# Late modulation joined to the attention, a gate column copied out, conversions moved: an 8-core hybrid attention and mixture-of-experts block on Trainium2

## The reference, cut to what matters

```python
c_act = silu(c)
mod = c_act @ w_ada + b_ada                  # (B, 6*2048)
sh1, sc1, gt1, sh2, sc2, gt2 = split(mod, 6)
h = rmsnorm(x, g_attn) * (1 + sc1) + sh1
proj = h @ w_in
y_a = mixer_a(proj[..., :4608]) @ w_a_up     # three dilated window attentions
y_b = mixer_b(q, k, v of proj) @ w_b_up      # 16 query heads, 4 key heads, all 4096 keys
gates = sigmoid(proj[..., o4:] + b_gate)
x = x + gt1 * ((gates_a * y_a + gates_b * y_b) @ w_out)
h2 = rmsnorm(x, g_ffn) * (1 + sc2) + sh2
x = x + gt2 * moe(h2)                        # 64 experts, 8 per token, one shared
return rmsnorm(x, g_final)
```

## Time and profile before

| | us |
|---|---|
| median of 3 runs | 6872.43 |
| lowest and highest of them | 6843.43, 7095.51 |
| the profiled execution, its own time | 6879.52 |
| its span, from the first to the last instruction of the slowest core (core 1) | 6877.3 |
| spans of the other cores | 6774.1 to 6874.5 |

### The profile page before, as it was taken

How to read it: one execution, slowest core, us unless ns; L and a number is a source line. 1 busy time by engine, 2 the same in 40 slices (tenths; PEclk the granted TensorE clock), 3 DMA queues, 4 the chain that set the end, 5 groups by cost and what they waited for, 6 DMA issues and landing times.

```text
span 6877.3 us, 64218 instructions; the slowest of 8 cores (6774.1 to 6877.3 us)
## 1 busy us (share of the span) xinstructions
PE 3962.4 (58%) x19194; PEld 1888.4 (27%) x19194; DVE 2186.1 (32%) x3834; ACT 2115.5 (31%) x3327; POOL 484.0 (7%) x607
## 2 busy tenths in 40 slices
PE   0103766765763887897895654555444545436545
PEld 0102333332331333343442322222222222213221
DVE  3444444546553322321213442122212212212212
ACT  0012553544561777784111211111111112112111
POOL 0000000000000000001110000001011101101113
PEclk9999877877886999998997776777776777767766
DMA  7653466465753244246755279899899997999987
GB/s 198 193 180 130 100 118 107 101 131 109 128 122 61 56 78 89 54 87 88 69 51 108 57 154 198 177 178 198 171 187 206 191 190 166 187 195 197 190 169 241
DMA packets 357433, 964.68 MB, mean 140 GB/s; under 512 B 139568, under 2 KB 187696, under 8 KB 336560
## 3 DMA queue, kind: packets, MB, share of 16 engines
q0 software_dynamic: 285232, 692.81, 56.8%
q1 hardware_dynamic: 71552, 263.97, 11.7%
HBM read 1372.53 MB, written 192.73 MB: 228 GB/s over the span
## 4 chain that ended last, share of the span: by engine, by line
DMA 35%; PE 34%; DVE 10%; issue 10%; ACT 7%; PEldq 3%; DVEq 1%; POOLq 0%; POOL 0%; ACTq 0%; PEld 0%; SPq 0%; another core or an unknown queue 0%
DMA idle<-e_bias 22%; PE psum L508 9%; DMA arena<-w_ada 4%; PE psum L1496 4%; PE psum L1467 3%; DMA arena<-w_in 3%; PE psum L956 3%; PE psum L958 3%; PE psum L1048 3%; PE psum L943 3%; PEldq L170 3%; DVE arena L465 2%; DMA arena<-yrows,arena 2%; ACT arena L463 2%; DVE arena L394 2%
## 5 line engine op out<-in xcount | busy, mean ns | idle before, releaser
L508 PE MATMUL psum<-arena 128*128 128x512 bf16 (+1 forms) x3648 | 925.7, 417 | 334.8 <-DVE arena L581 101.9
L1496 PE MATMUL psum<-arena 128*128 128x512 bf16 x1456 | 459.7, 486 | 530.7 <-DVE arena L1485 530.7
L1467 PE MATMUL psum<-arena 128*128 128x512 bf16 x2912 | 647.9, 382 | 12.0 <-ACT arena L1451 10.4
L946 ACT ACTIVATE arena<-psum 128x512 bf16<-128x512 f32 x1024 | 603.4, 597 | 102.3 <-PE psum L943 56.6
L508 PEld LDWEIGHTS psum<-arena 128*128 128x128 bf16 (+1 forms) x3648 | 383.4, 107 | 831.9 <-issue 500.1
L1448 PE MATMUL psum<-arena 128*128 128x128 bf16 x1456 | 169.7, 308 | 698.1 <-issue 545.6
L1471 ACT ACT_TABLE_LOAD x88 | 112.9, 1283 | 1271.7 <-PE psum L1467 1271.7
L956 PE MATMUL psum<-arena 128*128 128x512 bf16 x1024 | 405.1, 396 | 100.0 <-ACT arena L946 99.8
L443 ACT ACTIVATE arena<-arena 128x2048 bf16<-128x2048 f32 x102 | 194.1, 1903 | 727.6 <-DMA arena<-xr 504.7
L958 PE MATMUL psum<-arena 128*128 128x512 bf16 x1024 | 403.9, 394 | 0.0
L943 PE MATMUL psum<-arena 128*128 128x512 bf16 x1024 | 402.7, 395 | 0.0
(11 more groups left out here) (182 smaller groups left out, 4983.0 us busy)
## 6 DMA issues: line engine op xcount, KB each, us to landing
arena<-w POOLq DMA_DIRECT2D x129, 2048.0 KB, 36.5
wcast<-w POOLq DMA_DIRECT2D x63, 2048.0 KB, 13.5
arena<-wcast POOLq DMA_DIRECT2D x63, 2048.0 KB, 40.9
arena<-w_ada SPq DMA_DIRECT2D x128, 768.0 KB, 4.8
arena<-xr SPq DMA_DIRECT2D x78, 1024.0 KB, 6.1
yrows<-arena SPq DMA_DIRECT2D x91, 512.0 KB, 10.9
arena<-w_in POOLq DMA_DIRECT2D x15, 2048.0 KB, 45.9
arena<-w_in POOLq DMA_DIRECT2D x32, 512.0 KB, 7.1
```

Source lines behind the costliest of these rows:

```text
L508: ins = e.matmul(po[0:n, :], lhsT=hT_ap[:, k, 0:n], rhs=wv[:, k, :], start=(k == 0), stop=(k == 15))
L946: P.op("act", lambda e: e.activation(out=ptb[pi], in_=pbank(sbk), func=AF.Exp, scale=SCALE), reads=[PB[sbk]], writes=[ptb_t[pi]])
L1467: ins = e.matmul(pbank(bank), lhsT=xgT[g][:, k, :], rhs=wv_[:, k, :], start=(k == 0), stop=(k == 15))
L1496: ins = e.matmul(pbank(b2), lhsT=hidT[h][:, fc, :], rhs=wv_[:, fc, cs], start=(fc == 0), stop=(fc == 3))
```

## The change

The modulation is cut at the columns: the first 4096 are computed at the start, the other 8192 during the attention of mixer B.

- **At the start** (`mod_first`): 32 chunks of 128 x 2048 (1 MB) in four staging buffers, then a sum of 32 products. The first two own tiles' `produce_a1` stand ahead of it. The own tiles are then produced with `a1` two tiles ahead and no chunk between them.
- **During the attention** (`late_parts`): 16 groups of 512 columns, each 16 parts of 128 x 512 (256 KB), in two staging buffers and two accumulators. The parts are put at 256 per 1000 steps; at every 14th step (`si % 14 == 0`) a finished group is summed by four products in bank 6. `A2` follows after the attention.
- **Conversions**: the 13 of the key tiles are put by tile 23, the 30 of the attention by step 880.
- **Further blocks**: the gate column is copied to `gcol[4]` right after the gather, and the tile `hidT[0]`, in which it lies, is free for the rest.

```diff
-    stg_t = [T("stg0"), T("stg1")]
+    acc = V(BIG, [128, 4096], F32)
+    stg = [V(BIG + 16384 + i * 8192, [128, 2048], F32) for i in range(4)]
+    stg_t = [T("stg%d" % i) for i in range(4)]
...
-    def mod_chunk(half, k, pc):
+    def mod_part(bufs, bufs_t, a, a_t, k, col0, n):
...
+        P.dma("sp", "dx", st, w_ada[k * 128:(k + 1) * 128, col0:col0 + n], writes=[bufs_t[i]])
...
-    def mod_finish(half):
+    def mod_sum(a, a_t, c0, n, bank):
...
-            for j in range(48):
+            for j in range(n):
...
+    def mod_first():
+        for k in range(16):
+            for pc in range(2):
+                mod_part(stg, stg_t, acc[:, pc * 2048:(pc + 1) * 2048], t_acc, k, pc * 2048, 2048)
+        mod_sum(acc, t_acc, 0, 32, 7)
...
+    own_a1 = [produce_a1(xr[1024 + j * 128:1024 + (j + 1) * 128, :], 128) for j in range(2)]
+    mod_first()
     for j in range(8):
-        produce(xr[1024 + j * 128:1024 + (j + 1) * 128, :], 128, hT_own[:, :, j * 128:(j + 1) * 128], hto_t[j])
-        mod_h2_step(8)
+        produce_a2(own_a1[j], hT_own[:, :, j * 128:(j + 1) * 128], hto_t[j])
+        if j + 2 < 8:
+            own_a1.append(produce_a1(xr[1024 + (j + 2) * 128:1024 + (j + 3) * 128, :], 128))
...
-            cast_early(20 + (j + 1) * 13 // 32, [t_kb[j]])
+            cast_early(20 + min(13, (j + 1) * 13 // 23), [t_kb[j]])
...
+    def late_parts(upto, sums):
+        while late[0] < min(upto, 256) and late[0] // 16 < late[1] + 2:
+            cc, k = late[0] // 16, late[0] % 16
+            mod_part(late_stg, late_stg_t, late_acc[cc % 2], late_acc_t[cc % 2], k, 4096 + cc * 512, 512)
+            late[0] += 1
+        if sums and late[1] < late[0] // 16:
+            cc = late[1]
+            mod_sum(late_acc[cc % 2], late_acc_t[cc % 2], 32 + cc * 4, 4, 6)
+            late[1] += 1
...
-            cast_early(33 + (kvh * 256 + si + 1) * 30 // 1024, [ptb_t[si % 4]])
+            cast_early(33 + min(30, (kvh * 256 + si + 1) * 30 // 880), [ptb_t[si % 4]])
+            late_parts((kvh * 256 + si + 1) * 256 // 1000, si % 14 == 0)
...
+    while late[1] < 16:
+        late_parts(256, True)
...
+        P.op("dve", lambda e: e.tensor_copy(out=gcol[4], in_=gate_of(x, xgf)), reads=t_xgf, writes=[gcol_t[4], hidT_t[0]])
...
-        step_D(x, 1, gate_of(x, xgf), t_xgf, y, [xgT_t[0]])
+        step_D(x, 1, gcol[4], [gcol_t[4]], y, [xgT_t[0]])
```

More of the change, by code:

```diff
@@ L384, in mod_chunk @@
         stg_i[0] += 1
[L385 to L388, removed]
+        st = bufs[i]
+        P.dma("sp", "dx", st, w_ada[k * 128:(k + 1) * 128, col0:col0 + n], writes=[bufs_t[i]])
         if k == 0:
[L390 to L396 removed]
@@ L398, in mod_finish @@
-    def mod_finish(half):
-        pm = pbank(7)
+            P.op("dve", lambda e: e.tensor_scalar(out=a, in0=st, scalar1=c_act[:, 0:1], scalar2=None, op0=ALU.mult),
+                 reads=[bufs_t[i], t_cact], writes=[a_t])
+        else:
+            P.op("dve", lambda e: e.scalar_tensor_tensor(out=a, in0=st, scalar=c_act[:, k:k + 1], in1=a, op0=ALU.mult,
+                                                         op1=ALU.add),
+                 reads=[bufs_t[i], t_cact], writes=[a_t])
+    def mod_sum(a, a_t, c0, n, bank):
+        pm = pbank(bank)
@@ L401, in f @@
         def f(e):
             ins = None
-            for j in range(48):
-                ins = e.matmul(pm[:, j:j + 1], lhsT=acc[:, j * 128:(j + 1) * 128], rhs=ones_f[:, 0:1],
+            for j in range(n):
+                ins = e.matmul(pm[:, j:j + 1], lhsT=a[:, j * 128:(j + 1) * 128], rhs=ones_f[:, 0:1],
                                start=True, stop=True)
             return ins
[L407 to L418, removed]
+        P.op("pe", f, reads=[a_t, t_const], writes=[PB[bank]])
+        P.op("dve", lambda e: e.tensor_tensor(out=modT[:, c0:c0 + n], in0=pm[:, 0:n], in1=bada_pl[:, c0:c0 + n],
+                                              op=ALU.add),
+             reads=[PB[bank], t_const], writes=[t_modT])
@@ L419, in build_nc @@
     B1 = modT[:, 0:16]
     B2 = modT[:, 48:64]
[L422 to L436, removed]
+    def mod_first():
[3 more added lines that the diff above has]
+        mod_sum(acc, t_acc, 0, 32, 7)
+        P.op("dve", lambda e: e.scalar_tensor_tensor(out=A1, in0=modT[:, 16:32], scalar=1.0, in1=gattn,
+                                                     op0=ALU.add, op1=ALU.mult),
+             reads=[t_modT, t_const], writes=[t_A1])
@@ L907, in build_nc @@
     alias(t_ob, xt_t + xn_t + htt_t)
+    late_stg = [V(206336 + i * 2048, [128, 512], F32) for i in range(2)]
+    late_acc = [V(206336 + 4096, [128, 512], F32), V(EPB + 2048, [128, 512], F32)]
+    late_stg_t = [T("lstg0"), T("lstg1")]
+    late_acc_t = [T("lacc0"), T("lacc1")]
+    alias(late_stg_t + [late_acc_t[0]], prev_kv_tiles)
+    alias([late_acc_t[1]], [ring_t[2]])
+    late = [0, 0]
+    def late_parts(upto, sums):
[7 more added lines that the diff above has]
+            late[1] += 1
     def q_tiles(kvh):
@@ L1125, in build_nc @@
     idxu = [V(SML + 436 + 4 * i, [128, 1], F32).bitcast(U32) for i in range(5)]; idxu_t = [T("idxu%d" % i) for i in range(5)]
-    gcol = [V(SML + 456 + 4 * i, [128, 1], F32) for i in range(4)]; gcol_t = [T("gcol%d" % i) for i in range(4)]
+    gcol = [V(SML + 456 + 4 * i, [128, 1], F32) for i in range(5)]; gcol_t = [T("gcol%d" % i) for i in range(5)]
     t_h2d = [T("h2d%d" % j) for j in range(8)]
```

13 lines of the change are left out of this document (7 added, 6 removed).

## The result

The changed kernel takes 6539.22 us, the median of 4 runs (6501.46 to 6721.42); beside it, on the same chip, the kernel before took 6983.97 (4 runs, 6843.43 to 7174.67). The ratio is 0.952 with a 95% interval of 0.940 to 0.963. The profiled executions took 6518.53 us after and 6879.52 before, 361 us less. The forecast was 6497 in a range of 6450 to 6590. In some executions the cores of one die, or of both, take longer at a lower granted clock; the ratios are of the other executions alone, and e14, which had none of those, is read from its undisturbed die.

What follows compares the result with a forecast made beforehand. The prediction took chunk loads with two buffers, DMA 77% busy, to bound the start, and PE the attention. Its terms sum to -382.5 us from the median of 6872.4, with 7 added for the profiled execution: 6497 us, range 6450 to 6590.

Steps and rivals of the forecast that it cites:

- The start (-358): Modulation and own tiles before the first projection: four buffers keep DMA full, tiles follow without chunks between; 358 us less.
- The tiles' cycle: Own tiles after the first sum: ACT and DVE work sets one tile every 9.0 us.
- the rotary wait: Start of the projections: PE waits about 5 us before its third, as rotary operations stand behind the last tiles on DVE.
- The first query slab (-27): Ahead of the attention: conversions end at tile 23, so the slab loads earlier and PE's 33.0 us wait falls to 5.5.
- the conversions in the attention (-7): In the attention: closer conversions let the second and third query slabs load earlier, shortening PE's waits; 7 us less.
- the end (-34): Behind the attention: block 0's slabs load early, the 37.3 us wait goes, some 6 us return later; 34 us less.
- The late sums (+27.5): In the attention: 64 products for the late columns add in full on PE; 27.5 us more.
- The late parts (+12): In the attention: parts' DMA lags only in the last group, while conversions run; 12 us more, bounds 0 and 166.
- Rival A: Attention: late parts bound it, landing in 6 to 7.5 us; attention 1024 us, total about 6550 to 6600; chance 0.15.
- The clock (+4): In the attention: products after late sums may run at PE's low clock; 4 us more, bounds 0 and 29.
- rival C: In the attention: PE loses its clock at every late sum; 25 us more, total 6522; chance 0.12.
- The gate column (0): Further blocks of the experts: one DVE copy of 0.2 us each, where DVE waited anyway; 0 us.

Runs made afterwards that it cites:

- e14: Changed kernel with six late-part buffers, sums 8 parts later, query slab loaded at step 192, parts spread by time: 6591.0, 6615.86, 6627.8 and 10921.31 us.
- e8: Changed kernel with two 1 MB staging buffers in the first modulation instead of four: 6559.78 us in one execution.
- e7: Kernel before with only the new spacing of the conversions, in key tiles and attention: 6809.44 us in the profiled execution.
- e3: Changed kernel without the attention's 30 conversions, those experts loading float32: 6585.8 us in the profiled execution, attention 926.1 us.
- best version: Changed kernel with six late-part buffers, sums 8 parts later, query slab loaded at step 192, attention's conversions done by step 768: 6432.85 us, ratio 0.934.
- e4: Changed kernel with six staging buffers for the late parts instead of two: 6477.78 us, ratio 0.940.
- e5: Changed kernel with each group's one-column sum put 8 parts later, still two late-part buffers: 6532.16 us in one execution.

## Why the prediction was right or wrong

- **The start (-358).** Right in mechanism; the term mis-sized is the DMA rate. I took 295 GB/s of 306; 48.3 MB by source size from 25 to 167 us are 340. I had scaled a rate measured at a partial share with two buffers up to full use, and two buffers in flight do not show full use: e8 has a share of 0.90 and waits. The Trainium skill, page "DMA: Bandwidth & Descriptors", section "Bandwidth", gives about 358 GB/s for each core while both cores of an HBM domain stream; worked out from that figure the 48.3 MB would be an estimated 135 us, and the trace, with 142, is near. The tiles' cycle (9.0, measured 8.7), the first sum (13.7, measured 13.8) and the rotary wait (5, measured 4.3) held.
- **The first query slab (-27), the conversions in the attention (-7), the end (-34).** Right together: 68 forecast, 70 in e7. The slab's wait fell from 33.0 to 6.9, the end's wait from 37.3 to nothing. The reason given for the -7 holds in the mean of the cores: 5.7 us of it in e7 are shorter slab waits.
- **The late sums (+27.5).** Mis-sized a little: 23.3 on core 4. I had priced them from the 20.61 us of the first sum, which PE did from idle; without a wait ahead of it a late sum can take about half:

```profile
2136.70 1.83 PE L400 MATMUL psum<-arena 128*128 128x1 f32 x8 [32.73 <-DVE arena L390]
...
2874.39 0.95 PE L400 MATMUL psum<-arena 128*128 128x1 f32 x8
```

- **The late parts (+12).** The step that failed: "I estimate 3 us for 256 KB between conversions and 5 beside one". The first was right (2.8 in e3), the second is 12 to 19 us, because a conversion of 4.2 MB of reading is under way on the same 16 DMA engines and has two thirds of their time in the stretch shown. The Trainium skill, page "DMA: Bandwidth & Descriptors", section "Issuing engines are not separate DMA queues", says that transfers started by any engine run on the same 16 DMA engines and interleave; the trace agrees, with a median of 15.1 us for the parts in that stretch. In the attention this costs 154 (1080.5 against e3's 926.1, the low clock in it), and it hides the 30 of slab waits: the three terms -7, +12 and +4 of the forecast are +124 in fact, inside the bound of 166 for the parts. Rival A, priced at 1024 us of attention where 1080.5 were measured, was nearest to the mechanism, but went by a mean of 4 us per part. The mean is not what decides: on core 4 the parts landed after 5.7 us on average, which by the forecast's own formula is 3.5 us per part and no delay in the first three groups. The bursts are.
- **The clock (+4).** Mis-sized: 22 to 24 us on core 4. That is near the 25 that rival C put on top, but by another mechanism. On this core the nine sums behind waits of 2.6 to 32.7 us took 1.83 to 1.84 us, at half clock, and the seven behind no wait or up to 1.6 us took 0.95 to 1.02; in e3 fifteen of sixteen did. It is the waits that cost the clock, which the late landings make, and not the sums: rival C falls. The forecast read the clock of the first projection at 629.9 from the products' length too; the granted clock of that stretch is given as 1.00.
- **The gate column (0).** This step failed too: -38. "I see no engine that waited for it" was written beside a page whose chain leads with `idle<-e_bias` 22%. I had read it as the experts' affair and had not asked which tile that DMA writes for, and who else writes that tile.
- **The total.** The errors cancel in great part: +110 in the attention; -23 at the start, -38 by the copy, about -16 of scatter in the experts, the rest between stages. That the total lay in the range is luck in part: the two largest errors had opposite signs and nothing to do with each other.

Open: in the best version the attention is still 38 us over e3's. 33 of them are idle time of PE (139 us against 106, means of the cores), nearly all in waits for DVE operations that stand among the late parts; on core 4 PE waits 36.2 us at the projections behind L570 of the rotary chain. That the order of DVE's list (Q) is what is left there is argued, not tested. The copy's 38 us rest on 8 executions against 3.

## What to carry to other kernels

Price a small load on the critical chain at what it takes while the largest transfer beside it runs, and give it as many buffers as cover that landing: the median (4.1 us) says nothing when every eighth part takes over 12 us. When a chain is led by a transfer that carries no data, ask which tile it stands for and who else could be its last writer; and when a wait of hundreds of microseconds goes, look at the DMA share before counting it as gain. A wait that vanishes because its engine now comes late elsewhere will come back with the next repair (the slabs in e4, the divisions in e5).

## What was unexpected of the hardware

A 256 KB load on SP's queue beside one conversion from HBM to HBM on POOL's took up to 18.8 us, with 43 of 254 over 10 us, where it takes 2.8 us alone (5.1 at most). The conversions of the attention slowed as well, from a median of 12.7 us (core 1) and 13.4 (core 4) to 15.9 and 19.0 (2048 KB written each). With four buffers of 1 MB the start read 340 GB/s, above the 306 that I had made from the trace of two. And sixteen short stretches of one-column products in a busy PE stream did not by themselves bring the clock down; only the waits of 2.6 to 32.7 us ahead of nine of them did, as behind the one of 32.73 us in the kernel after, where one product takes 0.63 us, against 0.38 at the full clock:

```profile
2139.20 0.63 PE L960 MATMUL psum<-arena 128*128 128x512 bf16 x1
```
